# Two of eight one-hot rows move to GpSimd, the triangular inverse gets its transpose from TensorE, and the work behind the last expert key is signalled and ordered anew

## What is computed

```python
def peer_ffn(xn, w_q, sub_keys, u, v):          # 8 heads, 2 x 128 sub-keys, top 16
    ...
        best, pos = lax.top_k(cand, PEER_TOPK)
        expert = jnp.take_along_axis(cand_idx, pos, axis=-1)
        g = jax.nn.softmax(best, axis=-1)
        act = jax.nn.gelu(jnp.einsum('td,thkd->thk', xb, u[expert]), approximate=False)
        return jnp.einsum('thk,thkd->td', (g * act).astype(xb.dtype), v[expert])
...
        h = h + peer_ffn(hn, ...)
    return rms_norm(h, norm_f_g)                 # end of the first layer
...
    h = _rmsnorm(x, norm_pre)                    # start of the second: a norm of a norm
    cols = h @ w_in
...
    L = jnp.where(strict, jnp.einsum("bhncd,bhnsd->bhncs", kb, k)
                  * jnp.exp(jnp.where(strict, diff, 0.0)), 0.0)
    sol = lax.linalg.triangular_solve(eye + L, rhs, left_side=True, lower=True,
                                      unit_diagonal=True)
```

## Time and profile before

| | us |
|---|---|
| median of 3 runs | 1471.51 (1470.42 to 1471.89) |
| the profiled execution, its own time | 1472.0 |
| its span | 1470.2 |
| busy PE / DVE / ACT / POOL | 1430.2 / 1011.8 / 733.6 / 98.3 |
| share of the span | 97% / 69% / 50% / 7% |
| mean share of DMA engines busy | 45.5% (main queue) |
| mean granted TensorE clock | 0.995 of full speed |

### The profile page before, as it was taken

One profiled execution on the slowest core, in us unless ns is written; L12 is line 12 of the kernel. 1 busy time (PEld: TensorE's weight loads), 2 busy tenths in 40 slices (PEclk: granted clock), 3 DMA queues, 4 the chain that ended last, 5 costly groups with the idle time before them and its releaser, 6 DMA issues.

```text
span 1470.2 us, 22385 instructions
## 1 busy us (share of the span) xinstructions
PE 1430.2 (97%) x8002; PEld 1229.4 (84%) x8002; DVE 1011.8 (69%) x1817; ACT 733.6 (50%) x1113; POOL 98.3 (7%) x112
## 2 busy tenths in 40 slices
PE   8998999999999999999999999999999999999998
PEld 8877878688788888888888888888889899888786
DVE  6577479899866666666666666666668564665565
ACT  5544322276555555555555555555555832465343
POOL 0052134400000000000000000000010100000000
PEclk9999999999999999999999999999999999999999
DMA  5432253111365555555565556555534432334442
GB/s 202 176 118 83 89 212 129 43 58 44 129 198 188 186 187 194 188 186 190 190 191 185 187 192 190 187 188 188 181 138 174 165 135 87 137 131 148 170 169 101
DMA packets 56297, 229.16 MB, mean 156 GB/s; under 512 B 6689, under 2 KB 6961, under 8 KB 47409
## 3 DMA queue, kind: packets, MB, share of 16 engines
q1 hardware_dynamic: 55776, 228.19, 45.5%
q10 hardware_dynamic: 464, 0.20, 0.0%
HBM read 226.27 MB, written 2.10 MB: 155 GB/s over the span
## 4 chain that ended last, share of the span: by engine, by line
PE 89%; DVE 4%; ACT 3%; DMA 2%; issue 1%; POOL 0%; ACTq 0%; DVEq 0%; POOLq 0%
PE ps L2206 23%; PE ps L2016 15%; PE ps L2195 13%; PE ps L1983 8%; PE ps L2193 8%; PE ps L1940 5%; PE ps L2181 4%; PE ps L2159 2%; PE ps L2191 2%; PE ps L2056 1%; DVE lo L1349 1%; ACT hi L863 1%; PE ps L1951 1%; PE ps L2317 1%; PE ps L2327 1%
## 5 line engine op out<-in xcount | busy, mean ns | idle before, releaser
L1558 DVE TENSOR_TENSOR lo<-raw,hi 128x1024 fp32r<-128x1024 f32 x238 | 290.9, 1222 | 62.7 <-ACT hi L1003 62.7
L2195 PE MATMUL ps<-x,hi 128*128 128x512 f32 x840 | 301.9, 398 | 0.0
L1003 ACT ACTIVATE hi<-raw 128x1024 fp32r<-128x1024 f32 x238 | 250.1, 1051 | 0.0
L2193 PE MATMUL ps<-x,lo 128*128 128x256 f32 x960 | 249.7, 281 | 0.0
L2016 PE MATMUL ps<-hi,x 128*128 128x512 f32 x704 | 225.9, 395 | 4.9 <-ACT big L1111 2.5
L1349 DVE TENSOR_TENSOR lo<-raw,hi 128x2048 fp32r<-128x2048 f32 x62 | 142.5, 2300 | 80.8 <-ACT hi L863 80.7
L2193 PEld LDWEIGHTS ps<-x,lo 128*128 128x128 f32 x960 | 181.6, 189 | 9.3
L2195 PEld LDWEIGHTS ps<-x,hi 128*128 128x128 f32 x840 | 157.8, 188 | 33.6
L1050 ACT ACTIVATE oi<-ps 128x256 f32<-128x256 f32 x120 | 46.2, 385 | 234.6 <-PE ps L2195 233.4
L2016 PEld LDWEIGHTS ps<-hi,x 128*128 128x128 f32 x704 | 133.0, 189 | 34.9 <-ACT big L1111 3.0
L2206 PE MATMUL ps<-hi,wh 128*128 128x512 f32 x496 | 154.2, 392 | 3.6 <-DVE wl L1568 2.6
(11 more groups left out here) (382 smaller groups left out, 2157.9 us busy)
## 6 DMA issues: line engine op xcount, KB each, us to landing
raw<-in_v_t SPq DMA_DIRECT2D x128, 512.0 KB, 3.5
raw<-in_u_t SPq DMA_DIRECT2D x126, 512.0 KB, 3.4
raw<-in_pieces SPq DMA_DIRECT2D x62, 1024.0 KB, 4.8
ring<-in_peer_w_q SPq DMA_DIRECT2D x4, 2048.0 KB, 9.5
big<-in_up SPq DMA_DIRECT2D x4, 2048.0 KB, 8.6
ring<-in_w_mem_kv SPq DMA_DIRECT2D x2, 2048.0 KB, 8.4
resid<-in_x SPq DMA_DIRECT2D x1, 1024.0 KB, 5.4
big<-in_mem SPq DMA_DIRECT2D x1, 1024.0 KB, 4.9
```

The source lines that it names most:

```text
L1003: act.activation(hi[:, which, par], raw[:, which, par], ACT.Copy).then_inc(hi_done[which], 1)
L1558: dve.tensor_tensor(lo[:, which, par], raw[:, which, par], hi[:, which, par].bitcast(F32), ALU.subtract).then_inc(lo_done[which], 1)
L2193: pe.matmul(first, u_lo[:, par, c], xh[:, c], start=False, stop=False)
L2195: ins = pe.matmul(both, u_hi[:, par, c], x2[:, :, c], start=False, stop=(c == KC - 1))
```

## The change

- **Softmax.** ACT's exponential stands ahead of the copy `mv1`, no longer behind it.
- **Build.** GpSimd writes the last two of the eight `hotB` rows (`POOL_ROWS = 2`), DVE five, ACT one. PE waits, ahead of each second half, for GpSimd's rows too.
- **Last key.** ACT and DVE write the last key's V parts (`hi`, `lo`) ahead of its activations' copy and addition.
- **Signal by tile.** PE signals `v_mm` after token tile 0 of the last `v_pass`, and again after tile 1. DVE adds both tiles, then multiplies both by the weights, and only then splits `dnq0`.
- **One power for both norms.** ACT sums squares already divided by 1024, those of `resid` for both tiles first. POOL forms EPS times (mean + EPS) plus the second mean, and takes one power for each tile; the first norm's own root is taken last, for the final residual.
- **Padding.** The first `keep_busy` has 28 rounds for 33, the one between the two tiles' transposes none for 7.
- **Inverse.** The product Z Y and DVE's subtraction for X are gone. PE transposes the new Z between the two tiles of the level's piece, and ACT copies it to X, at levels 1 to 5.

```diff
+POOL_ROWS = 2
...
+            pool.wait_ge(pickT_done, 2)
+            for g in range(NG):
+                if g >= GBUF:
+                    pool.wait_ge(g_mm, 2 * (g - GBUF) + 2)
+                for k in range(GRP - POOL_ROWS, GRP):
+                    at = slice(g * GRP + k, g * GRP + k + 1)
+                    ins = pool.tensor_scalar(hotB[:, g % GBUF, k], iota, chosenT[:, 1, at], chosenT[:, 2, at], ALU.is_equal, ALU.mult)
+                ins.then_inc(masks_then_pool_rows_done, 1)
...
             for n in range(NT):
...
-                link(rsqrt(rstd_x[:, x], mean_x[:, x], sumsq_x[:, x], D, half))
-                pool.tensor_tensor(rstd_x[:, x], rstd_x[:, x], rstd_f[:, f], ALU.mult).then_inc(rstd_done, 1)
+                pool.wait_ge(sumsq_done, 6 + n + 1)
+                link(pool.tensor_scalar(mean_f[:, one], meansq_f[:, one], EPS, None, ALU.add))
+                link(pool.tensor_scalar(mean_x[:, one], mean_f[:, one], EPS, None, ALU.mult))
+            for n in range(NT):
+                one = slice(n, n + 1)
+                pool.wait_ge(sumsq_done, 8 + n + 1)
+                link(pool.tensor_tensor(mean_x[:, one], mean_x[:, one], meansq_x[:, one], ALU.add))
+                pool.tensor_tensor(rstd_x[:, one], mean_x[:, one], mhalf[:, 0:1], ALU.pow).then_inc(rstd_done, 1)
+            pool.tensor_tensor(rstd_f, mean_f, mhalf[:, 0:NT], ALU.pow).then_inc(rstd_done, 1)
...
             for k, g in enumerate(("mk0", "mk1", "mv0", "mv1")):
+                if g == "mv1":
+                    act.wait_ge(soft_in, 1)
+                    e = best.rearrange("p n h k -> p (n h k)")
+                    act.activation(e, e, ACT.Exp).then_inc(soft_exp, 1)
                 out_group(g, mkv_new.rearrange("p a n -> p (a n)")[:, k * TILE:(k + 1) * TILE], ACT.Copy)
...
             def second_key(n, v_loads, u_loads, par, last=False):
+                if last and par:
+                    act.wait_ge(v_mm, n - 2)
+                    split_hi(V, v_loads, par)
...
+                if l < LEVELS - 1:
+                    act.wait_ge(z_transposed, l + 1)
+                    act.activation(flat(X), ps[:, 6:8, :].rearrange("p b n -> p (b n)"), ACT.Copy).then_inc(x_done, 1)
...
-                for k in range(1, GRP):
+                for k in range(1, GRP - POOL_ROWS):
...
+                if last and par:
+                    split_lo(V, n, par)
                 dve.wait_ge(lb_exp_then_rest_out, n + (1 - AHEAD))
...
-            piece_split_lo("dnq0")
-
-            dve.wait_ge(v_mm, NKEY)
-            for n in range(NT):
+            for n in range(NT):
+                dve.wait_ge(v_mm, NKEY + n)
                 for half in range(2):
                     part = resid[:, n, half * TILE:(half + 1) * TILE]
                     dve.tensor_tensor(part, part, ps[:, 4 + 2 * n + half, :], ALU.add).then_inc(peer_out, 1)
+            dve.wait_ge(x_then_norm_f_loaded, 32)
+            for n in range(NT):
                 dve.wait_ge(peer_out, 2 * n + 2)
-                dve.wait_ge(x_then_norm_f_loaded, 32)
                 dve.tensor_tensor(scaled2[:, n], resid[:, n], norm_f, ALU.mult).then_inc(hg_done, 1)
+            piece_split_lo("dnq0")
...
-                        dve.tensor_tensor(X[:, part], X[:, part], ps[:, 6 + n, :].rearrange("p (h c) -> p h c", h=DH), ALU.subtract).then_inc(x_done, 1)
...
+                    if half:
+                        pe.wait_ge(masks_then_pool_rows_done, g + 2)
...
+                    if last and tau == 0:
+                        ins.then_inc(v_mm, 1)
...
-            keep_busy(3, 33)
+            keep_busy(3, 28)
             pe.wait_ge(peer_out, 4)
-            transpose_by_tile(scaled2, lambda n: pe.wait_ge(scaled_done, 4 + n + 1), (0, 7, 3))
+            transpose_by_tile(scaled2, lambda n: pe.wait_ge(scaled_done, 4 + n + 1), (0, 0, 3))
...
-                        for th in range(DH * n, DH * n + DH):
-                            ins = pe.matmul(th_out(6, th), Z[:, th], Y[:, th], start=True, stop=True)
...
+                def transpose_new_z(tile):
+                    if tile and l < LEVELS - 1:
+                        pe.wait_ge(z_done, NT * l)
+                        for th in range(TH):
+                            ins = pe.transpose(th_out(6, th), Z[:, th], ident[:])
+                        ins.then_inc(z_transposed, 1)
```

More of the change, by code:

```diff
@@ L464, in build @@
         up_w = [up_store[:, k] for k in UP_PLACE]
-        sumsq_f, mean_f, rstd_f = (take_small(NT) for _ in range(3))
-        sumsq_x, mean_x, rstd_x = (take_small(NT) for _ in range(3))
+        meansq_f, mean_f, rstd_f = (take_small(NT) for _ in range(3))
+        meansq_x, mean_x, rstd_x = (take_small(NT) for _ in range(3))
         meansq_p, mean_p, rstd_p = take_small(2, NT), take_small(NT), take_small(NT)
@@ L1050, in second_key @@
                 act.activation(act_j, ps[:, par, T:2 * T], ACT.Copy).then_inc(lb_exp_then_rest_out, 1)
-                act.wait_ge(v_mm, n - 2)
-                split_hi(V, v_loads, par)
+                if not (last and par):
+                    act.wait_ge(v_mm, n - 2)
+                    split_hi(V, v_loads, par)
                 act.wait_ge(lb_in_then_sum, n + (1 - AHEAD))
@@ L1362, in _ @@
             dve.tensor_tensor(masks[:, 0:LEVELS], ge[:, 0:LEVELS], ge[:, 1:LEVELS + 1], ALU.subtract)
-            dve.tensor_copy(masks[:, LEVELS], ident[:]).then_inc(masks_done, 1)
+            dve.tensor_copy(masks[:, LEVELS], ident[:]).then_inc(masks_then_pool_rows_done, 1)
             piece_split_lo("hf0")
@@ L1560, in second_key @@
             def second_key(n, at, par, last=False):
+                if last and par:
+                    split_lo(V, n, par)
                 dve.wait_ge(lb_exp_then_rest_out, n + (1 - AHEAD))
                 dve.tensor_tensor(act_j, act_j, ps[:, par, 0:T], ALU.add).then_inc(lb_in_then_sum, 1)
-                split_lo(V, n, par)
+                if not (last and par):
+                    split_lo(V, n, par)
                 dve.wait_ge(gelu_done, n)
@@ L2310, in _ @@
                 pe.wait_ge(bt_done, l)
+                pe.wait_ge(x_done, l)
                 for n in range(NT):
-                    pe.wait_ge(x_done, NT * (l - 1) + n if l > 1 else 1)
-                    if l > 1:
-                        pe.wait_ge(x_done, 1 + NT * (l - 2) + n + 1)
-                        pe.wait_ge(z_done, NT * (l - 2) + n + 1)
                     for th in range(DH * n, DH * n + DH):
@@ L2335, in _ @@
                 piece = LEVEL_PIECES[l - 1]
+                def transpose_new_z(tile):
[3 more added lines that the diff above has]
+                            ins = pe.transpose(th_out(6, th), Z[:, th], ident[:])
+                        ins.then_inc(z_transposed, 1)
                 if piece[:-1] in FEATURES:
-                    feature_piece(piece)
+                    feature_piece(piece, transpose_new_z)
                 else:
@@ L2340, in _ @@
                         banks = [bank_for(f"{piece[:-1]}{n}") for n in range(NT)]
-                    token_piece(piece, banks, g2_done)
+                    token_piece(piece, banks, g2_done, transpose_new_z)
             pe.wait_ge(z_done, NT * (LEVELS - 1))
```

36 lines of the change are left out of this document (13 added, 23 removed).

## The result

| | before | after |
|---|---|---|
| median of four runs, us | 1471.7 | 1455.05 |
| lowest to highest | 1470.42 to 1471.90 | 1454.83 to 1455.93 |
| profiled execution (span), us | 1472.0 (1470.2) | 1454.83 (1453.1) |

The ratio is 0.989 with a 95% interval of 0.9873 to 0.9907: the change takes 16.7 us off by the medians, and 17.1 by the two profiled spans. 1456.0 was forecast.

A forecast was written before the change was run, and what follows sets the result against it. TensorE (PE), busy 97% of the span, was taken as the bound; 8.8 (softmax and build) + 1.2 + 1.8 + 3.7 = 15.5 us off the profiled 1472.0 gave 1456.5, 1456.0 as median; forecast range 1453 to 1459, chance 0.60.

The forecast's parts named there:

- Softmax, 1.9: Ahead of the build: earlier exponential moves transposes up 2.9 us, but mkv_keep's landing lets only 1.9 us arrive.
- Build, 6.9: One-hot build: with five rows VectorE nearly keeps TensorE's pace; 6.9 us forecast, 8.8 together with softmax.
- h: Build: VectorE's assumed delay for each GpSimd row, between 0 and 0.29 us, taken as 0.13; VectorE's group is 2.42 + 2h.
- the second rival: Build and norms: GpSimd's rows hide better, h under 0.1, its sum not held up by lo; 17.9 us, 1453.6; chance 0.05.
- The lock rival: Build: VectorE waits for GpSimd, h 0.2 to 0.29; softmax and build give 0 to 4.3 us, 1460.5 to 1464.8; chance 0.20.
- GpSimd's rows, 0.3 to 0.35: Build: GpSimd's two-pointer compare takes 0.3 to 0.35 us a row, 0.7 for two, against 2.66 available.
- The slow-compare rival: Build: GpSimd's pair of rows sets the pace; above 3.3 us a pair the kernel is slower; chance 0.05.
- 276.21: Before's profile: VectorE's 128x1024 product at 276.21 took 3.26 us for 1.23, as if waiting for GpSimd; sign for a lock.
- Last key, 1.2: End of key loop: V's lo ahead of the addition lets TensorE start its last pass 1.2 us earlier.
- Signal, order, powers, 1.8: Norms, last pass to second tile's transposes: 11.7 us for 13.49, a gain of 1.8.
- Inverse, 3.7: Inverse: eight matmuls fewer net per level save 0.89 us, only 0.1 at level 1 for a 0.8 wait; 3.7 in all.
- The clock behind the norms: Behind the norms: TensorE idles about 1 us more, yet the granted clock stays full, priced at 0.

The follow-up runs named there:

- the split store: Changed kernel with mkv_keep stored in two DMAs, three quarters behind mv0's copy and the last quarter behind mv1's: 1453.1 us, ratio 0.9882.
- The stages: Changed kernel with VectorE's rows, hotA or both left out in some build groups, numbers for GpSimd's pointers in some: GpSimd's row alone 0.78 us, 0.63 with numbers.
- the undone version: Changed kernel with the end of the key loop and the norms of before: 1457.02 us, ratio 0.9902.

## Why the prediction came out right, and where its steps were off

- **Softmax, 1.9: right, and the reason too, with one wrong line in it.** The landing of `mkv_keep` sets the start; the split store shows it. But I had TensorE's first chunks end at 288.1, 0.8 before ScalarE's row. They end at 284.84 in after (286.4 in before's positions, which lie 1.5 later there), and TensorE waits 2.54. I had taken the chunks' length from before, where they ran at the lower clock level for most of it (4.44 us for 2.76). Had the store not been late, this error would have decided (argued; no run shows it).
- **Build, 6.9: 7.78 in B.** The direction of the disturbance was wrong. I let VectorE wait for GpSimd (h = 0.13 for each row); it is GpSimd that waits for VectorE. VectorE's `hotA` takes 1.15 us and its rows start 0.256 apart beside GpSimd as without it, 2.43 a group, so h is about 0. Nothing of the build is lost, as in the second rival; 7.6 was forecast for h = 0. (The lock rival's upper gain was mis-summed: by its own rule, 30 groups of 2.82 from 291.3 end at 375.9, that is 5.2 us and not 4.3.)
- **GpSimd's rows, 0.3 to 0.35: wrong by a factor of four.** The nearest row, the select with its 0.29, was no measure. A compare with two pointers takes 0.78 by itself, and one `hotA` in each group puts about 1.0 on the pair. The slow-compare rival, with 3.3 us for a pair as its threshold, was much nearer than its 0.05: the pair takes 2.65 with no idle time, and three rows, at 3.25, are slower than before (1475.0). The sum stayed right only since GpSimd still kept TensorE's pace of 2.65. That was luck.
- **The lock, rival at 0.20.** The Trainium skill's "SBUF — State Buffer", section "SBUF: two separate sides", says that a VectorE operation with two SBUF inputs or in a two-port mode locks GpSimd out while it runs, and that a GpSimd operation that starts first blocks VectorE in the same way. The stages agree for the two inputs (1.03 of the 1.07 us that were left of `hotA`), and the single-input operations that record 0.69 us for 1024 elements keep GpSimd out as well (0.49); which mode they ran in no trace tells. The reverse is what 276.21 shows, and the changed kernel repeats it: a VectorE product that takes 3.26 us, until 1.1 us behind the end of a GpSimd product of 3.26 us that had begun at 273.57.

```profile
274.66 3.26 DVE L1548 TENSOR_TENSOR big<-big 128x1024 f32<-128x1024 f32 x1
```

With GpSimd's short rows the reverse doesn't show. With three rows `hotA` starts at 303.54 while a row runs until 303.90, records the usual 1.23 us, and the next row on VectorE starts 1.14 behind it. There the page's rule and the measurement differ. My mistake was to carry 276.21 over from a long operation to short ones.
- **Last key, 1.2: 0.39 in D, of which the undone version shows 0.35.** The step "ACT's gelu comes 0.3 earlier and DVE's product follows it" was right up to the product, which ends at 1059.2. Left out was ScalarE's wait for TensorE ahead of `wh`: the buffer is read by the last pass but one until 1060. With a buffer of its own the missing 0.79 appears.
- **Signal, order, powers, 1.8: 1.31 in E**, 1.58 at its shorter value. From the last pass to the second tile's transposes it is 12.2 us (1061.08 to 1073.24) for the 11.7 of the sum. GpSimd was held up by VectorE as foreseen, but more often: L791 took 1.33 and 2.11 us and L792 1.03 for 0.2 each when alone. With that `lo` out of the way E gives 0.9 to 1.2 more, where I had said 1.3.
- **Inverse, 3.7: 3.70**, with a wait at level 1 of 0.58 for 0.8 forecast, and 10.01 to 10.26 us for the other levels, where I had 10.0 for each.
- **The clock behind the norms** stayed at 2.4 GHz, as assumed, in this execution; in the one with three rows it fell there, and E is 12.67. It wasn't at 2.4 everywhere in the profile I worked from: the 1.54 us at 91 us and the chunks at 286 us were in plain sight in the windows, and I didn't look there.
- **The sum**, 15.5, meets 15.6 by stretches more closely than its terms deserve. B and C gave 1.3 more than forecast, D and E 1.3 less. C's 0.43 lies within what C varies by where nothing was edited, so it isn't the change's. And the profiled executions differ by 17.1 us only since the clock gave 1.5 of them at 91 us.

## What to carry to other kernels

Before work is moved to an idle engine, run one instruction of that very form there, beside what the neighbour does: here the price was 0.78 us alone and 1.3 in company, for a guess of 0.3, and of the 2 us in each group that looked free none was left. When a chain is shortened, list all semaphores of each instruction in it, not only the one that came last in the profile; the buffer's wait was written in the code. And compare two kernels stretch by stretch between common instructions: single times moved by 1.5 us for reasons that no edit had.
